# Expert blocks that move only the rows of slots holding a token: bounded gathers, and one indirect store per block

## Chip, cores and metric

One Trainium2 chip, one core of it. The metric is device microseconds of one execution of the whole program; the kernel before takes 5017.96 us (median of 3 runs, 5016.63 to 5023.91).

## The reference, cut to what matters

A small network of two blocks runs on 512 tokens plus 16 meta tokens (T = 528 rows of 1024 floats). The first block has two layers, and each ends in a hierarchical mixture of experts. A token picks one of 4 groups and in it 2 of 8 experts. Everything is float32.

```python
order = jnp.argsort(flat_e)                       # T * 2 assignments, by expert
padded = (counts + MOE_BLOCK - 1) // MOE_BLOCK * MOE_BLOCK
dest = (pends - padded)[se] + jnp.arange(T * TOP_K) - starts[se]
row_tok = jnp.zeros((n_rows,), jnp.int32).at[dest].set(flat_tok[order])
xb = h[row_tok].reshape(n_blocks, MOE_BLOCK, D)
yb = (silu(xe @ w1[e]) * (xe @ w3[e])) @ w2[e]    # per block, one expert e
y = jnp.zeros((T, D)).at[row_tok].add(yb * row_gate[:, None])
```

A slot that no token took has gate 0, so what its row holds does not reach the result.

## The kernel before, in words

`moe` runs once per layer, in three steps: `route`, `experts`, `combine`. The kernel's blocks are 64 slots (SLOT), not 128; NBLK is 48 and ROWS is 3072.

**route.** Two stages. The first transposes h into rows, stores them in DRAM as `h_rows` (L1297) and computes the router's logits. The second picks experts on VectorE and makes `dest`, the slot of each of a token's two assignments. GpSimd scatters token numbers to `row_tok` in DRAM with 12 indirect DMAs (L1384), SP reads `row_tok` back into `slots`, one column per block (L1393), and VectorE works out each block's expert (`owner`) and the number of block pairs (`pairs`).

**experts.** One stage, a loop over pairs of blocks on every engine; z is 0 for the even and 1 for the odd block of a pair, and every buffer exists twice, once for each z.

- SP loads `w1`, `w3` (L1520, L1521) as soon as the buffer's last user, the up product two blocks earlier, is done, and `w2` (L1523) after the down product two blocks earlier. 3 loads of 1 MB per block.
- GpSimd copies a column of `slots` into `e_idx` (L1541), waits for the copy, and gathers the block's 64 rows of `h_rows` into `x[z]` (L1526, in `fetch`). It waits for nothing but the transpose that frees `x[z]`, so each gather is issued two blocks before its rows are transposed.
- TensorE, for block k: up products (L1565, 32 matmul records), then it waits for the gather of block k+1 and transposes those rows (L1552), then it waits for VectorE's product `e_hid`, transposes it (L1576), and multiplies by `w2` (L1584, 8 records). Its queue is in order, so a late gather of block k+1 also holds back the down product of block k.
- ScalarE: Silu (L1606), then the copy of the transposed rows of block k+1 (L1596), then the copy of the transposed hidden rows (L1612). After both blocks of a pair it issues four plain stores of `e_y` to `y_rows`, two per block (L1617).
- VectorE: the product `e_hid` (L1631) and the copy of the result out of PSUM into `e_y` (L1637).

The semaphore `x_in` says that a gather has landed, `x_turned` that its rows are transposed, `y_kept` that `e_y` is written, and `y_out` that a store has landed.

**combine.** GpSimd gathers the two result rows of each token from `y_rows` (L1654), 88 tokens at a time; VectorE weights and adds them; TensorE turns them back.

In `build` (L2512, L2524) `y_rows` and `row_tok` are cleared once, at the start. At the end of a stage SP clears the stage's semaphores, and GpSimd resets those used by its own DMAs.

Of the kernel before, what the change touches and what calls it, by code (L numbers as in the profile page):

```python
# [16 lines left out]
P = 128  # L17
# [3 lines left out]
T = SEQ + META  # L21
# [1224 lines left out]
def moe(k, a, li):  # L1246


    nc, ps = k.nc, k.ps
    NR = GROUPS + EXPERTS  # L1250
    with ExitStack() as tmp:
        def sb(name, shape, dt=F32):
            return k.sb(name, shape, dt, stack=tmp)
        gate = sb("gate", [TC, 2, NC1])
        dest = sb("dest", [TC, 2, NC1], I32)
        slots = sb("slots", [SLOT, NBLK + 1], I32)
        owner = sb("owner", [1, NBLK], I32)
        pairs = sb("pairs", [1, 1], I32)
        with ExitStack() as rt:
            route(k, a, li, rt, gate, dest, slots, owner, pairs, NR)  # L1260
        with ExitStack() as ex:
            experts(k, a, li, ex, slots, owner, pairs)
        with ExitStack() as cb:
            combine(k, cb, gate, dest)
    with ExitStack() as ln:
        st = k.sb("ln2_st", [P, T], stack=ln)
        sc = k.sb("ln2_sc", [P, KD, T], stack=ln)
        g, b = COL1["ln2_g"], COL1["ln2_b"]
        layer_norm(k, k.h, k.par1[:, g:g + KD], k.par1[:, b:b + KD], k.h, sc, st[:, :])


def route(k, a, li, rt, gate, dest, slots, owner, pairs, NR):
    nc, ps = k.nc, k.ps

    def sb(name, shape, dt=F32):
        return k.sb(name, shape, dt, stack=rt)
# [4 lines left out]
    tri = sb("before", [TC, TC])  # L1281
    iota = sb("iota", [TC, 64])
    tok = sb("tok_id", [TC, NC1], I32)

    with k.stage("router_landed", "logits_made", "h_turned", "h_kept", "h_stored", "lg_chain") as (
            block, landed, made, turned, kept, stored, steps):
        @block.sync
        def _(sp):
            sp.dma_start(w[:, :, :], a["router"][bass.ds(li, 1), :, :].rearrange(
                "a (t p) n -> p (a t) n", p=P)).then_inc(landed, 16)  # L1290
            sp.dma_start(wb[:, :], a["router_b"][bass.ds(li, 1), :]).then_inc(landed, 16)
            sp.dma_start(tri[:, :], a["k_tri"][:, 0, :]).then_inc(landed, 16)
            sp.dma_start(iota[:, :], a["k_iota"]).then_inc(landed, 16)
            sp.dma_start(tok[:, :], a["k_tok"]).then_inc(landed, 16)
            for j in range(NC1):
                sp.wait_ge(kept, j + 1)
                sp.dma_start(k.h_rows[j * TC:(j + 1) * TC, :], rows[:, j, :]).then_inc(stored, 16)  # L1297
            sp.wait_ge(stored, 16 * NC1)

        @block.tensor  # L1300
        def _(pe):
            for j in range(NC1):
                if j >= 3:
                    pe.wait_ge(kept, j - 2)
                for f in range(KD):
                    last = pe.transpose(ps[0:TC, 2 * (j % 3) + f // 4, (f % 4) * P:(f % 4 + 1) * P],
                                        k.h[:, f, j * TC:(j + 1) * TC], k.ident)
                last.then_inc(turned, 1)
            pe.wait_ge(landed, 16 * 5)
            for j in range(NC1):  # L1310
                o = ps[0:TC, 6, j * NR:(j + 1) * NR]
                for f in range(KD):
                    pe.matmul(o, lhsT=k.h[:, f, j * TC:(j + 1) * TC], rhs=w[:, f, :],
                              start=(f == 0), stop=False)
                last = pe.matmul(o, lhsT=k.ones[0:1, 0:TC], rhs=wb[:, :], start=False, stop=True)
            last.then_inc(made, 1)

        @block.scalar
        def _(act):
            for j in range(NC1):  # L1320
                act.wait_ge(turned, j + 1)
                b = 2 * (j % 3)
# [27 lines left out]
    with k.stage("g_shifted", "g_exp", "e_shifted", "e_exp", "counted", "ranked", "dest_made",  # L1350
# [39 lines left out]
        @block.sync  # L1390
        def _(sp):
            sp.wait_ge(scattered, 16 * 2 * NC1)
            sp.dma_start(slots[:, 0:NBLK], k.row_tok.rearrange("(b s) o -> s (b o)", s=SLOT),  # L1393
                         allow_slow_non_contiguous=True).then_inc(slots_in, 16)
            sp.wait_ge(slots_in, 16)

        @block.vector
        def _(dve):
# [73 lines left out]
def experts(k, a, li, ex, slots, owner, pairs):  # L1472
# [4 lines left out]
    def sb(name, shape, dt=F32):  # L1477
        return k.sb(name, shape, dt, stack=ex)
# [8 lines left out]
    y = [sb(f"e_y{z}", [P, D // 2]) for z in Z]  # L1487
    low, high = slice(0, SLOT), slice(SLOT, P)
    idx = [sb(f"e_idx{z}", [SLOT, 1], I32) for z in Z]
    d1 = a["moe_w1"].rearrange("l e (p t) n -> (l e) p t n", p=P)  # L1490
    d3 = a["moe_w3"].rearrange("l e (p t) n -> (l e) p t n", p=P)
    d2 = a["moe_w2"].rearrange("l e (p t) n -> (l e) p t n", p=P)
    names = ["up_w", "down_w", "idx_set", "x_in", "x_turned", "x_kept", "up", "silu", "hidden",
             "down", "y_kept", "y_out", "hid_turned", "hid_kept"]
    with k.stage("passed_gp", "passed_pe", "passed_act", *[f"{n}{z}" for n in names for z in Z]) as (
            block, passed_gp, passed_pe, passed_act, *sems):
        (up_w, down_w, idx_set, x_in, x_turned, x_kept, up, silu, hidden, down, y_kept,
         y_out, hid_turned, hid_kept) = [sems[2 * i:2 * i + 2] for i in range(len(names))]

        def turns(eng):  # L1500
            return eng.Fori(0, eng.value_load(pairs[0:1, 0:1], min_val=1, max_val=NBLK // 2))
# [23 lines left out]
        def fetch(gp, z):  # L1525
            gp.indirect_dma_start(  # L1526
                out=x[z][:, :], out_offset=None, in_=k.h_rows[:, :],
                in_offset=bass.IndirectOffsetOnAxis(ap=idx[z][:, 0:1].bitcast(U32), axis=0)
            ).then_inc(x_in[z], 16)

        @block.gpsimd
        def _(gp):
            gp.tensor_copy(idx[0][:, :], slots[:, 0:1]).then_inc(idx_set[0], 1)
            gp.wait_ge(idx_set[0], 1)
            fetch(gp, 0)
            with turns(gp) as i:
                for z, column, freed, count in ((1, 2 * i + 1, i + 1, i + 1), (0, 2 * i + 2, i + 2, i + 2)):
                    gp.wait_ge(x_turned[z], freed)  # L1540
                    gp.tensor_copy(idx[z][:, :], slots[:, bass.ds(column, 1)]).then_inc(idx_set[z], 1)  # L1541
                    gp.wait_ge(idx_set[z], count)
                    gp.sem_inc(passed_gp, 1)
                    fetch(gp, z)

        @block.tensor
        def _(pe):
# [41 lines left out]
        @block.scalar  # L1589
        def _(act):  # L1590
            credit(act, x_kept)
            for z in Z:
                act.sem_inc(y_out[z], 32)

            def keep_rows(z):
                act.activation(xt[z][:, :, :], ps[:, z, :].rearrange("p (f n) -> p f n", f=KD),  # L1596
# [5 lines left out]
            with act.Fori(0, n_turns) as i:  # L1602
                for z in Z:
# [7 lines left out]
                    act.wait_ge(hid_turned[z], i + 1)  # L1611
                    act.activation(hid_t[z][:, :, :], ps[:, 2 + z, EH:EH + 2 * SLOT].rearrange(  # L1612
                        "p (t n) -> p t n", t=2), ACT.Copy).then_inc(hid_kept[z], 1)
                for z in Z:
                    act.wait_ge(y_kept[z], i + 2)
                    for c, half in enumerate((low, high)):
                        act.dma_start(k.y_rows[bass.ds((2 * i + z) * SLOT, SLOT), c * 512:(c + 1) * 512],  # L1617
                                      y[z][half, :]).then_inc(y_out[z], 16)

            for z in Z:  # L1620
                act.wait_ge(y_out[z], n_turns * 32 + 32)
            act.sem_inc(passed_act, 1)

        @block.vector
        def _(dve):
            credit(dve, hidden, y_kept)
            with turns(dve) as i:
                for z in Z:
# [4 lines left out]
                                      si[z][high, :].rearrange("s (q t) -> s q t", t=2),  # L1633
                                      ALU.mult).then_inc(hidden[z], 1)
                    dve.wait_ge(down[z], i + 2)
                    dve.wait_ge(y_out[z], i * 32 + 32)
                    dve.tensor_copy(y[z][:, :], ps[:, 4 + z, :]).then_inc(y_kept[z], 1)  # L1637


# [846 lines left out]
def build(nc, a):  # L2486
    k = Kernel(nc)
    with k.top:
# [16 lines left out]
        k.y_rows = nc.dram_tensor("y_rows", (ROWS, D), F32, kind="Internal").ap()  # L2505
        k.row_tok = nc.dram_tensor("row_tok", (ROWS, 1), I32, kind="Internal").ap()
        k.y_cleared = k.top.enter_context(nc.semaphore("y_cleared"))
        k.pool_dma_sems("scattered", "x_in0", "x_in1", "y0_in", "y1_in")
        with k.stage("const_landed") as (block, landed):
            @block.gpsimd  # L2510
            def _(gp):
# [5 lines left out]
            def _(sp):  # L2517
# [2 lines left out]
                         (k.par2, "par2")]  # L2520
                for dst, src in loads:
                    sp.dma_start(dst[:, :], a[src]).then_inc(landed, 16)

                sp.dma_start(k.row_tok, a["k_zero_rows"]).then_inc(landed, 16)  # L2524
                sp.wait_ge(landed, 16 * (len(loads) + 1))
        k.ones_d, k.ones_h, k.ident = k.ones_d[:, :], k.ones_h[:, :], k.ident[:, :]
        first_block(k, a)
        second_block(k, a)
# [171 lines left out]
```

## Time and profile before

| | |
|---|---|
| median of 3 runs | 5017.96 us (5016.63 to 5023.91) |
| the profiled execution | 5006.6 us |
| its span in the profile | 5004.8 us |
| mean granted TensorE clock | 0.864 |
| busy: PE, PEld, DVE, ACT, POOL | 3664.7, 2368.3, 1670.4, 795.3, 278.8 us |
| expert blocks run | 64 (32 in each layer) |
| bytes read and written in HBM | 384.00 MB, 37.97 MB |

How to read it: PE is the matmul part of TensorE and PEld its weight loads, DVE is VectorE, ACT is ScalarE, POOL is GpSimd, and SPq, ACTq and POOLq are the queues in which an engine issues DMAs. "L1565" is a line of the kernel. In a timeline a row gives the start in us from the span's start, the time it took, engine, line, operation and, in brackets, how long the engine had been idle and what ended that. The busy shares are averages over a program with many stages; the expert stages are two stretches of about 300 us each.

### The profile page before, as it was taken

Reading aid. Unit: us, or ns where it says so; the run is one execution under the profiler, and the core shown is the slowest. Engines: PE = TensorE matmul, PEld = TensorE weight load, DVE = VectorE, ACT = ScalarE, POOL = GpSimd, SP = SyncE. Lnnn points to the kernel's source line nnn. Section 1 sums busy time; section 2 is a strip of 40 time slices with the busy share of each in tenths; the row PEclk is TensorE's granted clock in tenths of the full one; section 3 lists DMA queues with packets and bytes.
Section 4 is the critical chain, followed back from the end, with each engine's and each line's share of the span. In section 5 each row is a group of like instructions: output and inputs, shape, how many; then the busy total and the mean of one; then the engine's idle time right before and its main releaser. Section 6 shows DMA issues by size and latency. Waiting matters only on the chain. (4 is left out here: it accounts for less than half of the span.)

```text
span 5004.8 us, 75918 instructions
## 1 busy us (share of the span) xinstructions
PE 3664.7 (73%) x31800; PEld 2368.3 (47%) x31800; DVE 1670.4 (33%) x2752; ACT 795.3 (16%) x1638; POOL 278.8 (6%) x444
## 2 busy tenths in 40 slices
PE   0787698647739877976477485888547778879978
PEld 0654598534428446975344233443235533334434
DVE  2244455321122435552111405651234410123321
ACT  1002222021210122221112200340221100000010
POOL 0000121011110002200111100000000000000000
PEclk9988799869869877998699787699769989889989
DMA  3200000139932000001599440001000011112221
GB/s 127 87 13 19 2 5 4 34 117 389 389 118 80 1 19 2 5 3 39 189 384 378 173 134 6 1 1 67 4 18 0 7 44 67 62 56 84 67 58 52
DMA packets 173633, 413.63 MB, mean 83 GB/s; under 512 B 36765, under 2 KB 107693, under 8 KB 144989
## 3 DMA queue, kind: packets, MB, share of 16 engines
q1 hardware_dynamic: 153325, 354.07, 19.5%
q0 software_dynamic: 9776, 38.56, 2.4%
q10 hardware_dynamic: 10240, 16.79, 1.0%
q8 instruction: 222, 3.64, 0.3%
q14 instruction: 70, 0.57, 0.0%
HBM read 384.00 MB, written 37.97 MB: 84 GB/s over the span
## 5 line engine op out<-in xcount | busy, mean ns | idle before, releaser
L209 PE MATMUL ps<-h,win 128*128 128x264 f32 x1216 | 275.9, 391 | 77.1 <-DMA win<-in_w_in 77.1
L209 PE MATMUL ps<-h_lat,wup 128*128 128x512 f32 x704 | 305.0, 597 | 21.5 <-DMA wup<-in_w_up 21.5
L209 PEld LDWEIGHTS ps<-h,win 128*128 128x128 f32 x1216 | 234.7, 193 | 118.1 <-DMA win<-in_w_in 77.8
L1565 PE MATMUL ps<-e_w,e_xt 128*64 128x256 f32 x2048 | 249.2, 398 | 48.2 <-DMA e_w<-in_moe_w 40.0
L1565 PEld LDWEIGHTS ps<-e_w,e_xt 128*64 128x64 f32 x2048 | 166.2, 145 | 168.2 <-issue 117.7
L209 PEld LDWEIGHTS ps<-h_lat,wup 128*128 128x128 f32 x704 | 134.9, 192 | 191.1 <-issue 169.3
L209 PE MATMUL ps<-h_lat,wm 128*128 128x512 f32 x384 | 171.3, 609 | 46.1 <-DMA wm<-in_w_in 46.1
L1584 PE MATMUL ps<-e_w,e_hid_t 128*64 128x512 f32 x512 | 154.5, 730 | 29.4 <-ACT e_hid_t L1612 29.4
L209 PE MATMUL ps<-ff_a,wdn 128*128 128x512 f32 x352 | 154.3, 602 | 28.7 <-DMA wdn<-in_w_down 28.7
L1631 DVE TENSOR_TENSOR e_hid<-ps,e_silu 64x256 f32<-64x256 f32 x64 | 38.9, 607 | 365.7 <-ACT e_silu L1606 365.7
L209 PEld LDWEIGHTS ps<-h_lat,wm 128*128 128x128 f32 x384 | 75.0, 196 | 141.9 <-issue 93.8
L1052 PE MATMUL ps<-inv,nt 48*48 48x48 f32 x3520 | 127.6, 206 | 4.9 <-issue 4.0
L1156 DVE COPY_PREDICATED inv<-level,ps 112x384 f32<-112x384 int32 x176 | 103.4, 588 | 78.7 <-PE ps L1052 69.9
L510 ACT ACT_TABLE_LOAD x11 | 14.1, 1283 | 715.3 <-PEq L145 704.2
L209 PEld LDWEIGHTS ps<-ff_a,wdn 128*128 128x128 f32 x352 | 68.0, 194 | 115.0 <-issue 85.5
L1637 DVE COPY e_y<-ps 128x512 f32<-128x512 f32 x64 | 44.3, 692 | 218.9 <-PE ps L1584 218.9
L1052 PEld LDWEIGHTS ps<-inv,nt 48*48 48x48 f32 x3520 | 107.1, 122 | 7.2 <-issue 5.6
L2201 PE MATMUL ps<-lf_s,after 128*128 128x512 f32 x24 | 20.4, 944 | 122.5 <-POOL lf_s L2194 122.4
L1041 PE MATMUL ps<-inv,by_bet 48*48 48x48 f32 x3520 | 103.4, 206 | 8.4 <-issue 3.6
L985 ACT ACTIVATE nt<-ps 112x192 f32<-112x192 f32 x220 | 72.9, 331 | 218.1 <-PE ps L1041 214.7
L567 PE MATMUL ps<-ab_pt,v_ab 128*64 128x512 f32 x168 | 96.8, 735 | 14.1 <-ACT ab_pt L638 14.1
L209 PE MATMUL ps<-y_branch,wm 128*128 128x512 f32 x192 | 90.4, 635 | 20.2 <-DMA wm<-in_w_branch 20.2
(507 smaller groups left out, 6723.8 us busy)
## 6 DMA issues: line engine op xcount, KB each, us to landing
e_w<-in_moe_w SPq DMA_DIRECT2D x192, 1024.0 KB, 13.8
wmod<-in_w_mod SPq DMA_DIRECT2D x24, 1024.0 KB, 12.8
wup<-in_w_up SPq DMA_DIRECT2D x22, 1024.0 KB, 7.6
y_rows<-e_y ACTq DMA_DIRECT2D x128, 128.0 KB, 7.8
win<-in_w_in SPq DMA_DIRECT2D x10, 1536.0 KB, 6.4
wm<-in_w_in SPq DMA_DIRECT2D x6, 2048.0 KB, 7.9
wdn<-in_w_down SPq DMA_DIRECT2D x8, 1408.0 KB, 6.9
wout<-in_w_out SPq DMA_DIRECT2D x8, 1024.0 KB, 4.7
```

Source lines behind the costliest of these rows:

```text
L209: last = pe.matmul(ps[0:rows, bank + off, 0:cols], lhsT=lhsT, rhs=rhs, start=(n == 0), stop=(n == len(pairs) - 1))
L510: act.activation(split2(stat[:, n, 0:cols]), ps[:, 2 * (n % 4):2 * (n % 4) + 2, 0:half], ACT.Sqrt, bias=k.eps(eps), scale=1.0 / width).the ...
L567: last = pe.matmul(ps[0:orows, 6 + bank, 0:qn], lhsT=val, rhs=pt[0:w, g % 2, n, q0:q0 + qn], start=(n == 0), stop=(n == len(grp["values"]) ...
L985: act.activation(nt[z][:, :, :], ps[0:R, bank_a(c), 0:RT * WC].rearrange("p (f n) -> p f n", f=RT), ACT.Copy).then_inc(x_kept[z], 1)
L1041: last = pe.matmul(ps[hw, a0, f * WC:(f + 1) * WC], lhsT=by_bet[z][hw, f, 0, :], rhs=inv[z][hw, 0, f, :], start=True, stop=True)
L1052: last = pe.matmul(ps[hw, a0, (RT + f) * WC:(RT + f + 1) * WC], lhsT=nt[z][hw, f, :], rhs=inv[z][hw, 1, f, :], start=True, stop=True)
L1156: dve.copy_predicated(inv[z][0:R, :, :, :], k.level[0:R, level, d:d + 2, None, :].to_broadcast([R, 2, RT, WC]), ps[0:R, a0, 0:2 * RT * WC] ...
L1565: last = pe.matmul(ps[half, 2 + z, 0:EH], lhsT=xt[z][:, f, :], rhs=w[:, f, :], start=(f == 0), stop=(f == KD - 1))
L1584: last = pe.matmul(ps[half, 4 + z, :], lhsT=hid_t[z][:, t, :], rhs=w2[z][:, t, c * 512:(c + 1) * 512], start=(t == 0), stop=(t == 1))
L1631: dve.tensor_tensor(hid[z][high, :].rearrange("s (t q) -> s q t", t=2), ps[high, 2 + z, 0:EH].rearrange("s (q t) -> s q t", t=2), si[z][hi ...
L1637: dve.tensor_copy(y[z][:, :], ps[:, 4 + z, :]).then_inc(y_kept[z], 1)
L2201: pe.matmul(ps[:, d, :], lhsT=after[d][:, :], rhs=lf_s[d][:, :], start=True, stop=True).then_inc(ahead, 1)
```

## The change

The read-back of `row_tok` is done twice, so that `slots` has 128 partitions. Slots with no token now hold the number 3072 (ROWS), written by a store from a GpSimd-set tile at the start of each layer's `route`; the clearing of `row_tok` in `build` is gone. The gather in `fetch` has a bound of T - 1 and leaves out rows whose number is beyond it. The four plain stores per pair in ScalarE's queue are gone. In their place GpSimd issues one indirect store per block from all 128 partitions of `e_y`, each a half row of 512 floats, with indices from a table `y_row` that VectorE makes in the stage's beginning. Before the loop GpSimd clears both `x` tiles and issues two small DMAs that give the first credit of `y_out`.

```diff
@@ route, first stage
+        @block.gpsimd
+        def _(gp):
+            gp.memset(blank[:, :], ROWS).then_inc(blank_set, 1)
         @block.sync
         def _(sp):
+            sp.wait_ge(blank_set, 1)
+            sp.dma_start(k.row_tok.rearrange("(p n) o -> p (n o)", p=P), blank[:, :]).then_inc(stored, 16)
...
-            sp.wait_ge(stored, 16 * NC1)
+            sp.wait_ge(stored, 16 * NC1 + 16)
@@ route, second stage
-            sp.dma_start(slots[:, 0:NBLK], k.row_tok.rearrange("(b s) o -> s (b o)", s=SLOT),
-                         allow_slow_non_contiguous=True).then_inc(slots_in, 16)
-            sp.wait_ge(slots_in, 16)
+            for half in (0, SLOT):
+                sp.dma_start(slots[half:half + SLOT, 0:NBLK], k.row_tok.rearrange("(b s) o -> s (b o)", s=SLOT),
+                             allow_slow_non_contiguous=True).then_inc(slots_in, 16)
+            sp.wait_ge(slots_in, 32)
@@ experts, fetch
                 in_offset=bass.IndirectOffsetOnAxis(ap=idx[z][:, 0:1].bitcast(U32), axis=0)
-            ).then_inc(x_in[z], 16)
+                bounds_check=T - 1, oob_is_err=False).then_inc(x_in[z], 16)
@@ experts, GpSimd
-            gp.tensor_copy(idx[0][:, :], slots[:, 0:1]).then_inc(idx_set[0], 1)
+            for z in Z:
+                gp.memset(x[z][:, :], 0.0).then_inc(blank_set, 1)
+            gp.wait_ge(blank_set, 2)
+            for z in Z:
+                gp.dma_start(y[z][:, 0:SLOT], a["k_zeros"][:, 0:SLOT]).then_inc(y_out[z], 16)
+            gp.iota(y_row[:, :], pattern=[[2 * SLOT, NBLK]], base=0, channel_multiplier=2).then_inc(row_made, 1)
+            gp.tensor_copy(idx[0][:, :], slots[0:SLOT, 0:1]).then_inc(idx_set[0], 1)
...
                     gp.wait_ge(idx_set[z], count)
                     gp.sem_inc(passed_gp, 1)
                     fetch(gp, z)
+                    done, block_no = 1 - z, 2 * i + 1 - z
+                    if z:
+                        gp.wait_ge(row_made, 2)
+                    gp.wait_ge(y_kept[done], i + 2)
+                    gp.tensor_copy(y_idx[done][:, :], y_row[:, bass.ds(block_no, 1)]).then_inc(y_idx_set[done], 1)
+                    gp.wait_ge(y_idx_set[done], i + 1)
+                    gp.sem_inc(passed_gp, 1)
+                    gp.indirect_dma_start(
+                        out=y_halves, out_offset=bass.IndirectOffsetOnAxis(
+                            ap=y_idx[done][:, 0:1].bitcast(U32), axis=0),
+                        in_=y[done][:, :], in_offset=None, bounds_check=2 * ROWS - 1,
+                        oob_is_err=False).then_inc(y_out[done], 16)
@@ experts, ScalarE
-                for z in Z:
-                    act.wait_ge(y_kept[z], i + 2)
-                    for c, half in enumerate((low, high)):
-                        act.dma_start(k.y_rows[bass.ds((2 * i + z) * SLOT, SLOT), c * 512:(c + 1) * 512],
-                                      y[z][half, :]).then_inc(y_out[z], 16)
@@ experts, VectorE
+            chain = Chain(dve, row_steps)
+            dve.wait_ge(row_made, 1)
+            chain(dve.tensor_scalar(y_row[high, :], y_row[high, :], float(1 - P), None, ALU.add))
+            chain(dve.tensor_scalar(past[:, :], slots[:, 0:NBLK], ROWS - 0.5, float(4 * ROWS), ALU.is_gt, ALU.mult))
+            dve.tensor_tensor(y_row[:, :], y_row[:, :], past[:, :], ALU.add).then_inc(row_made, 1)
@@ build
-        k.pool_dma_sems("scattered", "x_in0", "x_in1", "y0_in", "y1_in")
+        k.pool_dma_sems("scattered", "x_in0", "x_in1", "y_out0", "y_out1", "y0_in", "y1_in")
...
-                sp.dma_start(k.row_tok, a["k_zero_rows"]).then_inc(landed, 16)
-                sp.wait_ge(landed, 16 * (len(loads) + 1))
+                sp.wait_ge(landed, 16 * len(loads))
```

## Rows read from the trace of the kernel before

**Rows 1.** DMA queues between 1100 and 1385 us, most of layer one's expert stage.
```profile
DMA packets 19942, 110.27 MB, mean 387 GB/s; under 512 B 2836, under 2 KB 2836, under 8 KB 8340
q1 hardware_dynamic: 13056, 95.04, 85.6%
q0 software_dynamic: 2405, 7.87, 8.8%
q10 hardware_dynamic: 4480, 7.34, 7.4%
```

**Rows 2.** Timeline, 1180 to 1212 us: an odd block and the even one after it.
```profile
1187.48 3.67 PE L1565 MATMUL ps<-e_w,e_xt 128*64 128x256 f32 x32 [0.84 <-issue]
1191.09 0.71 PE L1552 MATMUL ps<-ident,e_x 64*128 64x64 f32 x8
...
1191.35 0.34 SPq L1520 DMA_DIRECT2D e_w<-in_moe_w  x1
...
1191.84 0.60 ACT L1596 ACTIVATE e_xt<-ps 128x512 f32<-128x512 f32 x1 [0.27 <-PE ps L1552]
1191.98 0.18 POOL L1541 COPY e_idx<-slots 64x1 int32 x1 [7.88 <-PE ps L1552]
...
1192.36 0.31 PE L1576 MATMUL ps<-ident,e_hid 64*128 64x64 f32 x2 [0.56 <-DVE e_hid L1631]
1192.70 0.28 ACT L1612 ACTIVATE e_hid_t<-ps 128x128 f32<-128x128 f32 x1 [0.26 <-PE ps L1576]
1192.85 4.25 ACTq L1617 DMA_DIRECT2D y_rows<-e_y  x4
1192.94 0.93 POOL L1526 DMA_INDIRECT e_x<-h_rows,e_idx  x1 [0.78 <-POOL e_idx L1541]
...
1193.12 1.94 PE L1584 MATMUL ps<-e_w,e_hid_t 128*64 128x512 f32 x8 [0.46 <-ACT e_hid_t L1612]
...
1195.10 0.69 DVE L1637 COPY e_y<-ps 128x512 f32<-128x512 f32 x1 [2.89 <-PE ps L1584]
...
1196.44 3.67 PE L1565 MATMUL ps<-e_w,e_xt 128*64 128x256 f32 x32 [1.38 <-DMA e_w<-in_moe_w]
...
1203.43 3.51 PE L1584 MATMUL ps<-e_w,e_hid_t 128*64 128x512 f32 x8 [0.46 <-ACT e_hid_t L1612]
```

**Rows 3.** First up products and last e_y copy of each layer; e_y copies together.
```profile
1101.50 5.00 PE L1565 MATMUL ps<-e_w,e_xt 128*64 128x256 f32 x32 [5.39 <-DMA e_w<-in_moe_w]
...
1402.85 0.69 DVE L1637 COPY e_y<-ps 128x512 f32<-128x512 f32 x1 [2.89 <-PE ps L1584]
...
2452.88 5.16 PE L1565 MATMUL ps<-e_w,e_xt 128*64 128x256 f32 x32 [5.85 <-DMA e_w<-in_moe_w]
...
L1637 DVE COPY e_y<-ps x64: 690/692/693, 1112.5 to 2757.1; 128x512 f32<-128x512 f32 x64
```

**Rows 4.** The gathers of e_x, whole span, min/median/max; landings of two other indirect DMAs.
```profile
L1526 POOL DMA_INDIRECT e_x<-h_rows,e_idx x66: 928/932/962, 1090.3 to 2735.5; - x66
DMA to landing us min/median/max: 3.9/7.8/8.8
...
c_y<-y_rows,dest POOLq DMA_INDIRECT x24, 5.9
...
row_tok<-tok_id,dest POOLq DMA_INDIRECT x24, 2.1
```

**Rows 5.** Around the stage: its beginning, GpSimd's other forms, the slots read, the stage's end.
```profile
1089.50 0.18 POOL L1535 COPY e_idx<-slots 64x1 int32<-64x1 int32 x1 [6.35 <-POOLq L145]
...
L2194 POOL COPY k_s<-k_c 128x512 f32 x12 | 7.3, 611 | 0.0
L2512 POOL DMA_DIRECT2D y_rows<-in_k_zeros x1 | 0.8, 819 | 0.9 <-PEq L143 0.9
...
DMA to landing us min/median/max: 3.7/3.7/3.8
...
1410.06 0.97 POOL L1654 DMA_INDIRECT c_y<-y_rows,dest  x1 [26.88 <-ACTq L143]
```

More of the change, by code:

```diff
@@ L1255, in moe @@
         dest = sb("dest", [TC, 2, NC1], I32)
-        slots = sb("slots", [SLOT, NBLK + 1], I32)
+        slots = sb("slots", [P, NBLK + 1], I32)
         owner = sb("owner", [1, NBLK], I32)
@@ L1283, in route @@
     tok = sb("tok_id", [TC, NC1], I32)
-    with k.stage("router_landed", "logits_made", "h_turned", "h_kept", "h_stored", "lg_chain") as (
-            block, landed, made, turned, kept, stored, steps):
+    blank = sb("no_token", [P, ROWS // P], I32)
+    with k.stage("router_landed", "logits_made", "h_turned", "h_kept", "h_stored", "blank_set", "lg_chain") as (
+            block, landed, made, turned, kept, stored, blank_set, steps):
+        @block.gpsimd
+        def _(gp):
+            gp.memset(blank[:, :], ROWS).then_inc(blank_set, 1)
         @block.sync
         def _(sp):
+            sp.wait_ge(blank_set, 1)
+            sp.dma_start(k.row_tok.rearrange("(p n) o -> p (n o)", p=P), blank[:, :]).then_inc(stored, 16)
             sp.dma_start(w[:, :, :], a["router"][bass.ds(li, 1), :, :].rearrange(
@@ L1489, in experts @@
     idx = [sb(f"e_idx{z}", [SLOT, 1], I32) for z in Z]
+    y_idx = [sb(f"e_y_idx{z}", [P, 1], I32) for z in Z]
+    y_row = sb("e_y_row", [P, NBLK], I32)
+    past = sb("e_past", [P, NBLK], I32)
+    y_halves = k.y_rows.rearrange("r (c n) -> (r c) n", c=2)
     d1 = a["moe_w1"].rearrange("l e (p t) n -> (l e) p t n", p=P)
@@ L1493, in experts @@
     names = ["up_w", "down_w", "idx_set", "x_in", "x_turned", "x_kept", "up", "silu", "hidden",
-             "down", "y_kept", "y_out", "hid_turned", "hid_kept"]
-    with k.stage("passed_gp", "passed_pe", "passed_act", *[f"{n}{z}" for n in names for z in Z]) as (
-            block, passed_gp, passed_pe, passed_act, *sems):
+             "down", "y_kept", "y_out", "hid_turned", "hid_kept", "y_idx_set"]
+    with k.stage("blank_set", "row_made", "row_chain", "passed_gp", "passed_pe", "passed_act", *[f"{n}{z}" for n in names for z in Z]) as (
+            block, blank_set, row_made, row_steps, passed_gp, passed_pe, passed_act, *sems):
         (up_w, down_w, idx_set, x_in, x_turned, x_kept, up, silu, hidden, down, y_kept,
-         y_out, hid_turned, hid_kept) = [sems[2 * i:2 * i + 2] for i in range(len(names))]
+         y_out, hid_turned, hid_kept, y_idx_set) = [sems[2 * i:2 * i + 2] for i in range(len(names))]
         def turns(eng):
@@ L1527, in fetch @@
                 out=x[z][:, :], out_offset=None, in_=k.h_rows[:, :],
-                in_offset=bass.IndirectOffsetOnAxis(ap=idx[z][:, 0:1].bitcast(U32), axis=0)
-            ).then_inc(x_in[z], 16)
+                in_offset=bass.IndirectOffsetOnAxis(ap=idx[z][:, 0:1].bitcast(U32), axis=0),
+                bounds_check=T - 1, oob_is_err=False).then_inc(x_in[z], 16)
         @block.gpsimd
         def _(gp):
-            gp.tensor_copy(idx[0][:, :], slots[:, 0:1]).then_inc(idx_set[0], 1)
+            for z in Z:
[5 more added lines that the diff above has]
+            gp.tensor_copy(idx[0][:, :], slots[0:SLOT, 0:1]).then_inc(idx_set[0], 1)
             gp.wait_ge(idx_set[0], 1)
@@ L1540, in _ @@
                     gp.wait_ge(x_turned[z], freed)
-                    gp.tensor_copy(idx[z][:, :], slots[:, bass.ds(column, 1)]).then_inc(idx_set[z], 1)
+                    gp.tensor_copy(idx[z][:, :], slots[0:SLOT, bass.ds(column, 1)]).then_inc(idx_set[z], 1)
                     gp.wait_ge(idx_set[z], count)
@@ L1591, in _ @@
             credit(act, x_kept)
-            for z in Z:
-                act.sem_inc(y_out[z], 32)
             def keep_rows(z):
@@ L1613, in _ @@
                         "p (t n) -> p t n", t=2), ACT.Copy).then_inc(hid_kept[z], 1)
-                for z in Z:
-                    act.wait_ge(y_kept[z], i + 2)
-                    for c, half in enumerate((low, high)):
-                        act.dma_start(k.y_rows[bass.ds((2 * i + z) * SLOT, SLOT), c * 512:(c + 1) * 512],
-                                      y[z][half, :]).then_inc(y_out[z], 16)
             for z in Z:
-                act.wait_ge(y_out[z], n_turns * 32 + 32)
+                act.wait_ge(y_out[z], n_turns * 16 + 16)
             act.sem_inc(passed_act, 1)
@@ L1635, in _ @@
                     dve.wait_ge(down[z], i + 2)
-                    dve.wait_ge(y_out[z], i * 32 + 32)
+                    dve.wait_ge(y_out[z], i * 16 + 16)
                     dve.tensor_copy(y[z][:, :], ps[:, 4 + z, :]).then_inc(y_kept[z], 1)
```

## The prediction

> **What bounds the kernel now.** I read the page's slices first: the two stretches of the expert stage are the only ones in which DMA stands at nine tenths or more throughout. So I asked for the DMA queues inside the first stretch. They moved 387 GB/s, and the three queues' packets took 85.6 + 8.8 + 7.4 = 101.8% of the sixteen engines' time [rows 1]: the transfers are saturated. SP's weight queue (q1) has most of it; the gathers of token rows (q0) take 8.8%, the plain stores of results (q10) 7.4%. Then I read the timeline of two blocks [rows 2]. TensorE comes second, not far behind: one block is 3.67 us of up products, 0.71 of turning the next block's rows, 0.31 of turning hidden rows and 1.94 of down products, with short waits between, and before the next up product it waits 1.38 us for weights. Last, the length of a block: the first e_y copy starts at 1112.5 and the last of layer one at 1402.85, 31 blocks later, so 290.35 / 31 = 9.37 us. In layer two the first up product and the last copy lie 2757.1 - 2452.88 = 304.2 us apart against 301.35 in layer one, so 2.9 / 31 = 0.09 more, 9.46. Mean 9.41 us [rows 3].
>
> **What it removes.** Each layer has 2 x 528 = 1056 used slots, against 32 x 64 = 2048 moved: 48.4% of the gathered and stored rows go. From rows 1 that is 0.484 x (8.8 + 7.4) = 7.8% of the DMA time. If DMA stayed the bound, a block would take 9.41 x (101.8 - 7.8) / 101.8 = 8.69 us. ScalarE's four issues per pair (4.25 us from first to last, waits included) [rows 2] go as well; they stood behind the last copy of their pair and before the next Silu, beside TensorE's work, so I give them nothing.
>
> **What it adds in the loop: a wait in GpSimd's queue.** This decides the case. Today GpSimd waits only for the transpose that frees x, 0.18 us after it in rows 2, and its gather has two blocks of time. In the changed loop the queue is: gather of block 2i+1, wait for y of block 2i, store, gather of block 2i+2, wait for y of block 2i+1, store. The gather of block k+2 is now queued behind the finished result of block k, and TensorE needs it in the middle of block k+1, before the down product of block k+1. That makes a loop of dependences through one block: y written, store issued, gather issued, gather landed, rows turned, down product, next y written. Its length is the new block time, if it is above 8.69. Let Y be the end of the e_y copy of block k.
>
> GpSimd's leg, Y to the start of the gather's issue. Wake-up about 0.15 (row: transposes end at 1191.80, copy starts at 1191.98); index copy 0.18; wait for it 0.78; the store's issue, which I put at 1.04, a little over the gather's 0.93 since it has 128 indices and not 64; 0.05; the second index copy 0.18; 0.78 again [rows 2]. Sum 3.16 us.
>
> Is there cover? The next up product can start right after the down product, which ends 0.73 before Y (0.04 to the copy's start, 0.69 of copy), and it takes 3.67: it ends at Y + 2.9. The gather is issued at Y + 3.16. So TensorE waits for the gather's whole latency, in every block.
>
> Gather's leg, issue to landing. It is 3.9 us at its shortest, at the head of a stage, and 7.8 us in the median, among saturated queues [rows 4], with 64 rows in each. After the change it has 33 rows, and the queue is neither empty nor saturated: SP issues the 2 MB of w1 and w3 for the block after the next at the end of the up product, so at Y + 3.1, right beside the gather. Bounds: 3.9 or somewhat less with fewer rows, and 7.8. Being at the start of a burst, it is as near to one row as to the other, so I take the middle, 5.85.
>
> TensorE's leg, landing to the next Y. Turning the rows 0.71, 0.03 to ScalarE's copy of 0.60, 0.04 to the copy of the hidden rows of 0.28, 0.14 to the down product of 1.94, 0.04 to the e_y copy of 0.69 [rows 2]. The hidden rows are ready long before and are turned beside ScalarE's copy. Sum 4.48 us.
>
> The clock. In rows 2 the same down product took 1.94 us at 1195 and 3.51 at 1203, where TensorE was granted 1.2 instead of 2.4 GHz. If TensorE stands idle about six us in each block it may get the lower level more often. On this path are the down product (up to 1.57 more) and the turning (up to 0.4): between 0 and 2.0 us. I take 0.5, a quarter of the blocks, since the same short down product was at the high level in most blocks now.
>
> Block: 3.16 + 5.85 + 4.48 + 0.5 = 14.0 us (estimate). Its DMA work, 8.69, fits within. The change per block is +4.59, times 31 blocks and 2 layers: **+285 us**.
>
> **The edits outside the loop, per layer.** Before the first gather GpSimd gets two clears of 64 x 1024 (nothing like it in the trace; one is between almost nothing and the 0.61 us of a 128 x 512 copy, doubled for its length; I take 0.8), two DMA issues of 0.82 and a short iota: 4.2 us together [rows 5]. The first gather starts at 1090.3 + 4.2 = 1094.5, lands 5.85 to 7.8 later, is turned and copied in 1.8, so the first up product starts at 1102.2 to 1104.1 instead of 1101.50 [rows 3]; in layer two somewhat more. Its weights cover the rest. I take +2. The second read of slots adds between its own issue of some 0.7 us and another whole 3.7 us landing [rows 5], beside which nothing lies: +1.5. At the end the last store leaves through GpSimd: 0.15 + 0.18 + 0.78 and then a landing between the 2.1 of the scatter and the 5.9 of the result gather [rows 4], and two more semaphores are reset; the whole handover is now 1410.06 - 1403.54 = 6.5 us [rows 5]. Bounds 0 and +5, I take +2. The three VectorE operations that make y_row, and the blank store, are hidden: the first y is 11 us into the stage, and TensorE has six chunks to turn before it needs the router's loads. Without that cover each would be under 2 us. The removed load in build lands with its neighbours behind the clearing of y_rows: 0 to -1. Together 2 x 5.5 - 1 = +10.
>
> Sum: 5006.6 (span 5004.8) + 285 + 10 = 5302 for an execution like the profiled one. That one stands 11.4 us under the median of the runs, so for a median I say **5313 us**.
>
> **Rivals.**
>
> *The saved bytes win.* If the gather came in time the block would fall to 8.69 (TensorE allows it: from first up to end of down product it took 7.6 us in the odd block of rows 2, and 8.9 in the even one at the high clock): 62 x -0.72 + 10 = -35, so 4983. For it speaks that DMA is saturated now, rows 1. Against it speaks the order in GpSimd's queue. It decides where the gather lands before the up product's end, that is with less than nothing left for it. 4%.
>
> *A short gather.* With idle engines and few rows only a fixed part could be left. The nearest row is the token scatter, 2.1 us [rows 4]. Then the block is 3.16 + 2.1 + 4.48 = 9.74, and the kernel 62 x 0.33 + 10 = +30, 5048. The gathers' own shortest, 3.9 us, speaks against it. 5%. The Trainium skill, "DMA: Bandwidth & Descriptors", section on the anatomy of a software-generated DMA, gives 2.0 us plus bytes over 436 GB/s, which for 33 rows of 4 KB is about 2.3 us (an estimate from that page); by that rule the gather's leg would be 2.3 and not 5.85, and the time 5061. The trace does not agree with it for 64 rows under load: 7.8 us.
>
> *The indices do not skip.* If rows out of bounds still cost a descriptor each, the gather keeps 64 rows and its 7.8 us: block 15.9, 62 x 6.5 + 10 = +413, 5431. The trace has no bounded DMA, so nothing speaks for or against. 8%.
>
> *All at the slow end.* Gather 7.8 and TensorE at 1.2 GHz throughout: 3.16 + 7.8 + 4.48 + 2.0 = 17.4, 62 x 8.0 + 10 = +506, 5524. 5%.
>
> **How the numbers follow.** 78% for the forecast's case, with its gather between 3.9 and 7.8 and its clock term between 0 and 1: 11.5 to 16.4 us. Without the corners, where both are at an end at once, 12.0 to 15.9, so +161 + 10 to +402 + 10, 5190 to 5430. The upper end just reaches the indices that do not skip. Faster by over 0.2% (about what a measurement of this kernel can tell from no change) 4%, within it 1%, slower 95%.
>
> **What would show it.** In the changed profile TensorE's largest idle time in the expert stage should be before L1552's transposes, ended by the DMA of e_x, some 6 us in each of about 62 blocks; GpSimd's new index copy should start right after each e_y copy and its gather 3.2 us behind; the DMA share in the stretch should fall from 101.8% to about two thirds; landings of e_x should be between 4 and 8 us; the start of a block should come every 14 us. I am wrong if e_x has landed before the up product ends, if blocks stay near 9 us, or if the DMA queues are still full.

## The result and the profile after

The changed kernel takes 5487.96 us (median of 6 runs, 5485.21 to 5501.06) against 5019.29 us for the kernel before: a ratio of 1.0936 (95% interval 1.0922 to 1.095). It is slower by 469 us, where 294 were forecast, and lies 58 us above the forecast range. The profiled execution took 5491.45 us, 485 more than that of the kernel before.

The page of the changed kernel, from its first line and parts 2 and 5, and behind it three lines of the page of the kernel before. In part 5 a group's columns are line, engine, operation, tiles, count, then busy us and mean ns, then the engine's idle time before the group and what ended it.

```profile
span 5489.7 us, 75951 instructions
...
PEclk9987898766666996998666668868977998989989
DMA  3200000165542100000355535000100002112221
...
L1582 PE MATMUL ps<-ident,e_x 64*128 64x64 f32 x528 | 68.7, 304 | 534.8 <-DMA e_x<-h_rows,e_idx 534.8
...
L1614 PE MATMUL ps<-e_w,e_hid_t 128*64 128x512 f32 x512 | 227.1, 1036 | 59.5 <-ACT e_hid_t L1640 59.5
```
```profile
PEclk9988799869869877998699787699769989889989
DMA  3200000139932000001599440001000011112221
...
L1584 PE MATMUL ps<-e_w,e_hid_t 128*64 128x512 f32 x512 | 154.5, 730 | 29.4 <-ACT e_hid_t L1612 29.4
```

Two things stand out. TensorE is idle for 534.8 us before the transposes of gathered rows, 8.4 us in each of the 64 blocks, and what ends it is the gather. And in the slices of the expert stage the DMA digit has fallen from 9 to about 5 while the granted clock has fallen from between 7 and 9 tenths to 6: the resource that bound the kernel is now partly idle, and TensorE is slower where it does work (1036 ns for a mean record of the down product, 730 before).

The timeline of one block of the changed kernel answers to [rows 2]; columns as there.

```profile
1256.83 4.22 PE L1595 MATMUL ps<-e_w,e_xt 128*64 128x256 f32 x32
...
1257.21 0.69 DVE L1665 COPY e_y<-ps 128x512 f32<-128x512 f32 x1 [10.79 <-PE ps L1614]
1258.07 0.18 POOL L1567 COPY e_y_idx<-e_y_row 128x1 int32 x1 [13.00 <-DVE e_y L1665]
1259.13 1.03 POOL L1570 DMA_INDIRECT y_rows<-e_y,e_y_idx  x1 [0.88 <-POOL e_y_idx L1567]
1260.16 0.20 POOL L1559 COPY e_idx<-slots 64x1 int32 x1
...
1261.21 0.99 POOL L1538 DMA_INDIRECT e_x<-h_rows,e_idx  x1 [0.85 <-POOL e_idx L1559]
1261.24 0.33 SPq L1532 DMA_DIRECT2D e_w<-in_moe_w  x1
...
1269.40 0.76 PE L1582 MATMUL ps<-ident,e_x 64*128 64x64 f32 x5 [8.35 <-DMA e_x<-h_rows,e_idx]
...
1270.52 0.60 ACT L1624 ACTIVATE e_xt<-ps 128x512 f32<-128x512 f32 x1 [9.06 <-PE ps L1582]
1271.02 0.27 ACT L1640 ACTIVATE e_hid_t<-ps 128x128 f32<-128x128 f32 x1
1271.43 3.68 PE L1614 MATMUL ps<-e_w,e_hid_t 128*64 128x512 f32 x8 [0.94 <-ACT e_hid_t L1640]
...
1275.15 0.69 DVE L1665 COPY e_y<-ps 128x512 f32<-128x512 f32 x1 [13.05 <-PE ps L1614]
```

This is the whole loop of dependences, from the end of one e_y copy (1257.90) to the end of the next (1275.84). GpSimd's leg to the gather's issue at 1261.21 is 3.31 us. The gather's leg to the transposes at 1269.40 is 8.19. TensorE's leg is 6.44, with the down product at the lower clock, 3.68 us. Together 17.94 us. SP issues w1 0.03 us after the gather.

The same three legs, read from the timeline for 62 blocks (31 in each layer), have these means: GpSimd 3.31 us, the gather 7.11 up to the transposes' start, TensorE 6.37, together 16.79. The length of the gather's leg goes with the order in which the transfers leave. In 16 of these blocks SP issued w1 0.57 to 0.86 us behind the gather, and the leg was 4.1 to 6.6 us, in the mean 5.6. In the 42 in which w1 left earlier than that, up to 0.55 us ahead of the gather, it was 6.8 to 9.6, in the mean 8.1. (The last two blocks of a layer have no new w1.)

Two answers about tiles of the changed kernel: the gathers' landings, and the e_y copies of layer one, with the first and last start.

```profile
DMA to landing us min/median/max: 2.1/7.6/9.5
```
```profile
L1665 DVE COPY e_y<-ps x32: 691/692/693, 1118.8 to 1638.6; 128x512 f32<-128x512 f32 x32
```

The mean block of layer one is (1638.6 - 1118.8) / 31 = 16.77 us; in layer two it is 16.80. Against 9.41 [rows 3] that is 62 x 7.37 = 457 us of the 485. The edges give 2 x 9.2 = 18 more, in three pieces of a layer: the second slots read (1.7 us from its issue to the next stage's first GpSimd instruction), the clears and the later first gather (2.7 us to the first up product), and the handover to combine (12.0 us from the last e_y copy to the first gather of results, 7.2 before). The remaining 10 us lie in untouched stages. These differ by as much between profiled executions: in wait_only below, which changes nothing ahead of its loop, the first gather is issued at 1099.9 us, and in the kernel before at 1090.3.

### The profile page after: what moved, and what is told of

Same layout as the page of the kernel before. It is cut to its first block and busy times, and to the rows that moved or that the text cites. A ratio compares the mean times of both kernels' runs of the same rounds, so it can differ in the third digit from the quotient of the medians.

```text
span 5489.7 us, 75951 instructions
## 1 busy us (share of the span) xinstructions
PE 3758.2 (68%) x31800; PEld 2409.8 (44%) x31800; DVE 1671.4 (30%) x2758; ACT 788.4 (14%) x1638; POOL 368.0 (7%) x584
## 5 line engine op out<-in xcount | busy, mean ns | idle before, releaser
L1582 PE MATMUL ps<-ident,e_x 64*128 64x64 f32 x528 | 68.7, 304 | 534.8 <-DMA e_x<-h_rows,e_idx 534.8
L1582 PEld LDWEIGHTS ps<-ident,e_x 64*128 64x128 f32 x528 | 58.5, 207 | 562.2 <-issue 475.2
L1595 PE MATMUL ps<-e_w,e_xt 128*64 128x256 f32 x2048 | 271.0, 423 | 1.7 <-ACT e_xt L1624 1.7
L1614 PE MATMUL ps<-e_w,e_hid_t 128*64 128x512 f32 x512 | 227.1, 1036 | 59.5 <-ACT e_hid_t L1640 59.5
L1595 PEld LDWEIGHTS ps<-e_w,e_xt 128*64 128x64 f32 x2048 | 187.6, 160 | 140.6 <-issue 95.4
L1624 ACT ACTIVATE e_xt<-ps 128x512 f32<-128x512 f32 x66 | 39.5, 598 | 564.2 <-PE ps L1582 564.1
L1614 PEld LDWEIGHTS ps<-e_w,e_hid_t 128*64 128x64 f32 x512 | 54.5, 214 | 142.1 <-issue 142.1
```

The costliest lines, as they stand in the source:

```text
L1582: last = pe.transpose(ps[:, z, f * SLOT:(f + 1) * SLOT], x[z][:, f * P:(f + 1) * P], k.ident[0:SLOT, 0:SLOT])
L1595: last = pe.matmul(ps[half, 2 + z, 0:EH], lhsT=xt[z][:, f, :], rhs=w[:, f, :], start=(f == 0), stop=(f == KD - 1))
L1614: last = pe.matmul(ps[half, 4 + z, :], lhsT=hid_t[z][:, t, :], rhs=w2[z][:, t, c * 512:(c + 1) * 512], start=(t == 0), stop=(t == 1))
```

## The experiments

The theory is that the place of the store in GpSimd's queue makes every gather wait for a result, and that the block is then the sum of three legs. The rivals: bounded gathers and indirect stores are slow by themselves; the clock is the cause; the rows or the weights' transfers set the gather's latency. Ten kernels were run. Unless it says otherwise, a diff is against the changed kernel and "block" is the mean of layer one, from the e_y copies' first and last start.

**wait_only** is the kernel before with the wait alone.

```diff
                     gp.wait_ge(x_turned[z], freed)
+                    gp.wait_ge(y_kept[z], i + 2 - z)
                     gp.tensor_copy(idx[z][:, :], slots[:, bass.ds(column, 1)]).then_inc(idx_set[z], 1)
```

> The kernel before with one thing of the change: GpSimd waits for the result of block k before it issues the gather of block k+2. Stores stay in ScalarE's queue, gathers keep all 64 rows. If the order in GpSimd's queue is the cause, a block is 1.2 us from the e_y copy to the gather's issue (the changed kernel's 3.3 without the store's 2.1), 7.8 for the gather, 6.2 for TensorE's leg at the lower clock: about 15.2 us against 9.41, so 62 x 5.8 = +360 on 5007, about 5365. If instead the indirect stores or the bounded gathers are what costs, neither is here and the time stays within 15 us of the kernel before.

Measured 5205.81 us, ratio 1.0369 (1.0348 to 1.039). The block is 12.3 us. So the wait costs 184 us without any bounded or indirect store in the kernel. But it was less than the 360 expected, and the landings say why.

```profile
DMA to landing us min/median/max: 3.9/5.1/8.7
L1638 DVE COPY e_y<-ps x32: 690/691/693, 1124.6 to 1506.4; 128x512 f32<-128x512 f32 x32
```
```profile
1260.55 0.93 POOL L1526 DMA_INDIRECT e_x<-h_rows,e_idx  x1 [0.78 <-POOL e_idx L1542]
...
1263.29 0.33 SPq L1520 DMA_DIRECT2D e_w<-in_moe_w  x1
...
1265.95 0.49 PE L1553 MATMUL ps<-ident,e_x 64*128 64x64 f32 x5 [2.91 <-DMA e_x<-h_rows,e_idx]
```

Here 64 rows land in 5.1 us in the median, less than the changed kernel's 7.6 with about half the rows. Without the store in front of it the gather is issued 2.74 us ahead of w1 in this block (1.6 to 2.9 in all), not beside it. That made the meeting with the weights the next suspect.

**weights_after** moves the weights out of the gather's way.

```diff
-                    sp.wait_ge(up[z], i + 1)
+                    sp.wait_ge(x_turned[1 - z], i + 1 + z)
                     sp.dma_start(w1[z][:, :, :], one(d1)).then_inc(up_w[z], 16)
```

> The changed kernel, but SP issues w1 and w3 only when the next block's rows have been gathered and turned, so that a gather never meets their 2 MB. If meeting them is what makes the gather slow (7.6 us in the median of the changed kernel, 5.1 where wait_only issued it some 2 us ahead of them), its leg falls to about 3.5 to 4.5 us, a block to about 13 (3.3 + 3.9 + 5.8), and the time to 5021 + 62 x 3.6 + 18 = 5260, 5200 to 5300. If the bounded gather is slow by itself, the time stays at 5488 or goes above it.

Measured 5276.02 us, ratio 1.0514 (1.0491 to 1.0537). The block is 13.19 us.

```profile
DMA to landing us min/median/max: 2.1/3.5/9.0
L1665 DVE COPY e_y<-ps x32: 690/692/692, 1123.7 to 1532.7; 128x512 f32<-128x512 f32 x32
```
```profile
1260.71 0.99 POOL L1538 DMA_INDIRECT e_x<-h_rows,e_idx  x1 [0.85 <-POOL e_idx L1559]
1264.39 0.77 PE L1582 MATMUL ps<-ident,e_x 64*128 64x64 f32 x5 [4.23 <-DMA e_x<-h_rows,e_idx]
...
1265.66 0.33 SPq L1532 DMA_DIRECT2D e_w<-in_moe_w  x1
```

The same bounded gather of the same rows now takes 3.5 us in the median. So 4.1 of its 7.6 us in the changed kernel were the weights beside it, by the medians. By the means of the gather's leg it is 3.5 (7.11 to 3.62), which is nearly all that the block lost; TensorE's leg stayed near its 6.37, at 6.28. Holding the weights back by some 5 us gave 212 us. A bounded gather is not slow by itself.

Its 3.5 us are not those of idle engines either. Here is what the DMA engines moved in each us from 1250 to 1290:

```profile
GB/s 0 0 0 131 377 401 410 426 442 360 434 285 154 37 0 0 131 197 418 426 451 401 369 418 299 213 152 0 0 0 147 385 401 426 459 418 377 426 254 115
```

The gather issued at 1260.71 comes while the engines still move 434 GB/s of other transfers, and by 1264 nothing is left. With nothing beside it a gather of no rows at all can be read in the changed kernel: the last one of a layer (1632.1 us) has only empty slots.

```profile
DMA to landing us min/median/max: 2.1/2.1/2.1
```

In all_rows below, the same gather with 64 rows took 4.1 us up to the transposes in layer one and 3.9 in layer two.

**awake** keeps TensorE busy in its wait, and **after_awake** does that on top of weights_after, with 4 in place of 6.

```diff
+                    rouse(k, pe, 6)
                     pe.wait_ge(x_in[1 - z], i * 16 + (32 if z else 16))
```

> The changed kernel with six dummy products of 128x512 on TensorE between the up product and the wait for the gather, which keep it busy for most of its idle time. If the lower clock behind the wait is part of the block time, the down product falls from 3.7 to 1.94 us and the turning by 0.3 in most blocks: 62 x -1.7 = -105, about 5385. If the clock only shifts waiting about, 5490 as in the changed kernel.

> weights_after (block 13.2 us, gather 3.5) with four dummy products in TensorE's wait, as awake had six. In awake the higher clock gave next to nothing back, and its gathers became slower (7.9 us). If that was because an up product that ends sooner lets the weights' 2 MB start sooner beside the gather, then here, where the weights wait, the whole of the down product's 1.7 us and the turning's 0.3 come back: 13.2 - 1.8 = 11.4 us per block, 5276 - 112 = 5165. If the clock is not on the path at all, 5276.

awake took 5487.6 us, ratio 1.093 (1.0907 to 1.0954): no change that these runs can tell, with an interval of 12 us to either side. The stretch from 1150 to 1400 us, first of the changed kernel, then of awake (busy time and count of each engine, granted clock, DMA share, GB/s):

```profile
1150.00:1400.00 250.00, 123.93 (x726) 67.44 (x724) 18.80 (x29) 24.96 (x49) 33.73 (x57) 0.70 0.55 193
```
```profile
1150.00:1400.00 250.00, 191.85 (x904) 95.03 (x905) 19.40 (x30) 25.71 (x51) 33.61 (x57) 0.88 0.58 201
```
```profile
1257.21 3.65 PE L1595 MATMUL ps<-e_w,e_xt 128*64 128x256 f32 x32
...
1261.05 0.33 SPq L1532 DMA_DIRECT2D e_w<-in_moe_w  x1
...
1261.53 0.99 POOL L1538 DMA_INDIRECT e_x<-h_rows,e_idx  x1 [0.85 <-POOL e_idx L1559]
1270.57 0.74 PE L1582 MATMUL ps<-ident,e_x 64*128 64x64 f32 x5 [4.37 <-DMA e_x<-h_rows,e_idx]
```

The clock did rise, 0.70 to 0.88. But in the block shown, where the up product ran at the higher clock, w1 left 0.48 us ahead of the gather and not behind it, and the gather took 9.04 us. The median landing rose from 7.6 to 7.9. In the means of 62 blocks TensorE's leg fell from 6.37 to 5.54 us and the gather's rose from 7.11 to 7.55, so the block lost 0.40 us and the loops 25. Two things lie behind the longer gather's leg: w1 left 0.2 us or more ahead of the gather in 34 of 58 blocks and not in 23, and in 15 of 62 blocks the dummy products ended after the landing, so that TensorE no longer waited for it. Besides, in the first block of each layer, whose next rows have long landed, the dummies stand in the way:

```profile
1118.21 5.42 PE L231 MATMUL ps<-h,ident 128*128 128x512 f32 x12
1123.56 0.52 PE L1582 MATMUL ps<-ident,e_x 64*128 64x64 f32 x5
```

From the first gather's issue to the first e_y copy this costs 4.8 us in layer one and 4.4 in layer two. The 16 us that are left are of the size of the interval, and the profiled execution is 11 us shorter than that of the changed kernel. So awake does not show that the clock is worth nothing; it shows that these dummies' gain is mostly used up elsewhere.

In after_awake, where the weights wait, the block fell from 13.19 to 12.51 us and the time to 5232.75 us, ratio 1.0436 (1.0412 to 1.046). That is 43 us and not the 112 expected. TensorE's leg fell by 1.16 us (6.28 to 5.12), and the gather's rose by 0.46 (3.62 to 4.08), though w1 and w3 waited. The reason for the rise was not isolated. One that fits: a shorter TensorE's leg brings the next gather nearer to the end of the transfers before it. Behind a leg under 5 us it took 4.3 us in the mean, behind a longer one 3.9. The clock is on the path, with 1.2 us of TensorE's leg and 0.7 us of the block as measured so; the full 1.8 was not shown.

**all_rows** leaves nothing out: all slots are moved, with row 0 of h in the empty ones.

```diff
-            gp.memset(blank[:, :], ROWS).then_inc(blank_set, 1)
+            gp.memset(blank[:, :], 0).then_inc(blank_set, 1)
```

> The changed kernel with 0 and not 3072 in the empty slots: every gather and store moves all of its rows, nothing is left out, and the order stays. If the number of rows hardly matters to a gather's latency, the time is within 20 us of 5488. If skipping is worth what half of the rows take (or if left-out rows cost more than moved ones), it moves by 50 us or more.

Measured 5566.76 us, ratio 1.1093 (1.1072 to 1.1115), so 79 us more than the changed kernel. The block is 17.82 us, 1.05 more, and the gather's median landing 8.7 us, 1.1 more. So skipping works, and half of the rows are worth about 1.1 us of a gather's latency, against 4.1 for the weights. This answers the rival in which rows out of bounds cost as much as others: its 5431 us lie nearer to the result than the forecast, but the rows were left out.

**late_store** keeps the whole change and moves only the store, behind the gather that follows in time. Step n of GpSimd's loop gathers block n and stores block n - 3 in place of n - 1; `store(buffer, column, count)` waits for `y_kept` at count, and its index table has two columns more in front; two steps after the loop store the last blocks, and VectorE clears e_y once, since the first store of each buffer has only indices out of bounds. **late_all_rows** is the same with 0 in the blank slots, as in all_rows.

```diff
+            gp.memset(y_row[:, 0:2], 4 * ROWS).then_inc(row_made, 1)
...
-                    done, block_no = 1 - z, 2 * i + 1 - z
...
-                    gp.wait_ge(y_kept[done], i + 2)
...
+                    store(1 - z, 2 * i + 1 - z, i + 1)
+            for z in Z:
+                store(z, 2 * n_gp + z, n_gp + 1)
```

> The changed kernel with each indirect store queued one pair later, behind the gather of block k+3, so that no gather waits for a result. If the order is the cause, a block falls to between 8.7 us (the saved rows shorten the transfers) and 9.4 (they don't), and with some 15 us outside the loops the time is 4970 to 5025. If indirect stores and bounded gathers cost by themselves, it stays above 5300.

> late_store with 0 in the empty slots: the order of late_store, all rows moved. If the saved rows are what took late_store's block from 9.41 to 8.9 us, the block goes back to about 9.4 and the time to 5011 + 62 x 0.53 = 5044, 5030 to 5055. If TensorE and not DMA sets the block, it stays at 5011.

late_store took 5011.53 us, ratio 0.9979 (0.9969 to 0.9988): the same DMAs in another order are 476 us faster than the changed kernel and slightly faster than the kernel before. Its block is 8.91 us. late_all_rows took 5043.02 us, ratio 1.0054 (1.0036 to 1.0071), with a block of 9.48. So the saved rows are worth 0.57 us per block in layer one; in layer two, where the blocks are 8.83 and 9.60, it is 0.77. The 0.72 of the forecast's rival was near. DMA queues of late_store (1110 to 1385 us), then of late_all_rows (1120 to 1385 us), to be read beside [rows 1]:

```profile
q1 hardware_dynamic: 13211, 96.22, 90.9%
q0 software_dynamic: 4963, 8.11, 8.9%
```
```profile
q1 hardware_dynamic: 11813, 86.03, 85.4%
q0 software_dynamic: 4438, 14.42, 16.2%
```

In both, GpSimd's queue has the same number of packets for the same weights: 4963 / 96.22 = 51.6 and 4438 / 86.03 = 51.6 per MB. But the bytes differ, 0.084 and 0.168 MB per MB, and so does the share of time. A row out of bounds keeps a packet, one of hardly any bytes or time: this queue's time per MB of weights is halved as its bytes are.

**one_block** is late_store with store n - 2 in step n. The gather of block k + 3 then waits for the result of block k + 1.

> late_store with the store one block earlier: the gather of block k+3 waits for the result of block k+1 at most, so a gather has a whole block more than in the changed kernel. It is then issued 3.3 us after an e_y copy and needed 2.9 + 8.9 us after it: 8.5 us for a gather of some 7.4. If lead time is all that counts, the block is 8.9 us as in late_store and the time 5005 to 5018. If any wait for a result in that queue costs, it is above 5060.

Measured 5005.67 us, ratio 0.9983 (0.9972 to 0.9994), with a block of 9.04. One block more of lead is enough. It is not quite free: in late_store TensorE's matmuls waited for a gather only at the head of each of the two stages, here 22 times.

**plain_store** takes out the indirect store and gives ScalarE its four plain stores back; the bounded gathers stay. **lean** is plain_store with one slots read, as before the change, and with VectorE in place of GpSimd clearing x.

```diff
-                    gp.indirect_dma_start(
...
+                for z in Z:
+                    act.wait_ge(y_kept[z], i + 2)
+                    for c, half in enumerate((low, high)):
+                        act.dma_start(k.y_rows[...], y[z][half, :]).then_inc(y_out[z], 16)
```
```diff
-            for z in Z:
-                gp.memset(x[z][:, :], 0.0).then_inc(blank_set, 1)
...
+            for z in Z:
+                dve.memset(x[z][:, :], 0.0).then_inc(blank_set, 1)
```

> The changed kernel with the results stored as before, four plain stores per pair in ScalarE's queue, all rows; only the bounded gathers, the sentinel and the second slots read stay. If the order is the cause and DMA time is the bound, a block is 9.41 x (101.8 - 4.3) / 101.8 = 9.0 us, so -25 and about +8 outside: 4985 to 5000. If bounded gathers are the cost, above 5200.

> plain_store with less around its loop: one read of slots, and VectorE and not GpSimd clears the x tiles, so that the first gather is issued ahead of the weights again. The block stays at 8.9 us. Of the first up product's delay (GpSimd's 1.9 us of clears, the second read's 1.7, the gather among the weights) about 5 us per layer come back: 5006 - 10 = 4996, 4988 to 5000, below the kernel before and below plain_store. If the start of the stage is hidden by the weights anyway, it stays at 5003 to 5009.

plain_store took 5006.0 us, ratio 0.9968 (0.9956 to 0.9981), block 8.93; lean 4993.33 us, ratio 0.9944 (0.9929 to 0.9959), block 8.94. lean beats both kernels, 24 us under the kernel before as run beside it. Half of the saving (the gathers') gives the whole shorter block: 8.93 with plain stores, 8.91 with skipping ones. Here is lean in a part of layer one, and then TensorE's up products in the whole of the kernel before, of late_store and of lean:

```profile
1150.00:1400.00 250.00, 197.87 (x1400) 116.02 (x1400) 36.38 (x56) 52.72 (x97) 30.65 (x53) 0.92 0.98 384
```

```profile
L1565 PE MATMUL ps<-e_w,e_xt 128*64 128x256 f32 x2048 | 249.2, 398 | 48.2 <-DMA e_w<-in_moe_w 40.0
```
```profile
L1601 PE MATMUL ps<-e_w,e_xt 128*64 128x256 f32 x2048 | 246.9, 395 | 14.4 <-DMA e_w<-in_moe_w 9.9
```
```profile
L1576 PE MATMUL ps<-e_w,e_xt 128*64 128x256 f32 x2048 | 252.1, 400 | 7.0 <-DMA e_w<-in_moe_w 3.4
```

In lean the DMA share is 0.98 where [rows 1] had 101.8%, so the transfers are still close to full. But TensorE hardly waits for weights any more: 3.4 us in the whole program, against 40.0 before. In late_store the same stretch has a DMA share of 0.96 and 368 GB/s against lean's 384, with the same length of a block. So the engines could have moved more, and the stores' bytes were saved with next to no time to gain from them. What comes next is then the chain of TensorE and ScalarE, which no run took apart. In every second block ScalarE loads a function table for 1.28 us before its Silu (15 times for 31 of them in late_store's first stretch); what that is worth stays open. And the late indirect stores lengthen the stage's end: from the last e_y copy to combine's first gather it is 12.0 us in late_store and 7.6 in plain_store.

## Why the prediction was wrong in size and right in kind

**The mechanism held.** The loop of dependences runs through y, store, gather, turning, down product, as forecast; the predicted signature (idle time before L1552's successor, ended by e_x; an index copy behind each e_y copy) is what the page shows. late_store moves one queue entry and gets 476 us back, and wait_only puts the wait into the old kernel and loses 184.

**GpSimd's leg** was put at 3.16 and is 3.31 us: the row-by-row sum holds within 5%, worth 62 x 0.15 = 9 us.

**Two terms of the sum failed, by about the same: the gather's leg and the clock.** Of the forecast block's 14.0 us against the measured 16.79, 1.26 are the gather's and 1.39 are TensorE's leg with its clock term.

**The gather's leg.** I wrote that it is "as near to one row as to the other, so I take the middle, 5.85". It is 7.11 us in the mean (7.6 in the median of the landings, 8.19 in the block shown), near the loaded end of the rows. The bounds were right; the choice between them was not. I had seen that SP issues 2 MB "right beside the gather", and treated that as half a load. weights_after shows that the meeting costs 3.5 us in the mean. In wait_only, where the gather leaves 1.6 to 2.9 us ahead of w1, its leg is 5.11 us in the mean, with all 64 rows. In [rows 4] the shortest landing belonged to gathers issued more than a microsecond ahead of the first weights, so it was not the near row. Fewer rows took only 1.1 us off (all_rows). The term is worth 62 x 1.26 = 78 us.

**The clock term** was 0.5 with bounds 0 to 2.0, since I took a quarter of the blocks to be at the lower level. The down product's mean record rose from 730 to 1036 ns on the page. TensorE's leg is 6.37 us in the mean against 4.48 + 0.5, and it is 6.0 or more in 60 of 62 blocks: nearly all of them, and not a quarter. So the term is 1.9 if all that the leg has above 4.48 is put down to the clock, close to its upper bound. It is worth 62 x 1.39 = 86 us. A longer wait and a lower clock came together, where I had put the case of both at their ends at 5% as a rival of its own, at 5524; the result is nearer to it than to the forecast.

**The short-gather rival** fell: even with w1 and w3 held back the gather took 3.5 us. The rule of the Trainium skill ("DMA: Bandwidth & Descriptors", anatomy of a software-generated DMA), 2.0 us plus bytes over 436 GB/s, makes 2.3 of it (an estimate); the measurement decides, and is 1.2 longer. The rule's fixed part has a row near it: the gather of no rows, with nothing beside it, landed in 2.1 us.

**The saved bytes** would have been worth 0.72 us per block by the DMA share. They are worth 0.57 and 0.77 in the late order. The block stops at 8.8 to 8.9 us and not at 8.69; there TensorE's waits for weights have fallen from 40.0 to 9.9 us, so its own chain is what comes next.

**The edges** were put at +5.5 per layer and are +9.2: slots 1.7 (1.5 forecast), the head 2.7 (2), the end 4.8 (2, bound 5).

**The range** left out the corners "where both are at an end at once", and let the clock term reach only 1. The two terms were not independent: both belong to the same wait. The measured block of 16.8 us lies beyond the 16.4 that the upper corner would have reached, because the clock term alone went beyond its 1.

## What to carry to other kernels

Before an operation moves to another queue, read what already stands in that queue and for whom: a store that waits for a result must not stand in front of a load that produces the next one. Put it behind every load that can be issued without it, here one block is enough. Price a small DMA that something waits for by its neighbours in time: the row to take is the one with the same large transfers issued at the same moment, even if the queues are half empty on average, and it is worth reading which of the two is issued first; and a term that comes from the same wait as another goes to its end together with it.

## What the runs showed that I had not expected

- A gather of some 33 rows of 4 KB took 3.5 us in the median with the next 2 MB of weights held back, and 7.6 us with them issued within a microsecond of it, though the DMA share over the stage was only 0.55.
- Half a microsecond in the order of two transfers went with 2.5 us of a gather's leg. In the changed kernel the gather's leg was 5.6 us in the mean where w1 left 0.57 to 0.86 us behind the gather, and 8.1 where it left earlier than that.
- A gather whose rows are all out of bounds landed in 2.1 us with nothing beside it; with 64 rows it took 3.9 and 4.1 us up to the transposes.
- 64 rows issued 1.6 to 2.9 us ahead of the same 2 MB landed in 5.1 us in the median.
- Raising TensorE's clock from 0.70 to 0.88 of its full speed in the stage changed the whole time by nothing that the runs can tell. TensorE's leg lost 0.83 us per block, the gather's gained 0.44, and the dummy products cost 4.8 and 4.4 us in the first blocks.
- A row out of bounds keeps its packet in an indirect DMA but nearly none of its bytes or time.
